# Down weights by output columns, the embedding's projection among the last quad's gate and up products

## The chip, the cores and the metric

The kernel runs on one core of one Trainium2 chip, in f32 throughout. The metric is device time in microseconds of one execution of the whole program.

## The reference

Two blocks follow each other on 256 tokens of width 1024. The first has two layers; the second, one layer with a recurrent unit, sparse attention and an MLP, is not touched. Cut to what the change bears on:

```python
def first_block(x, p, ...):
    for i in range(2):                                 # DEPTH
        h = rms_norm(x, norm_mix[i])
        q, k, v, cu, cg, ga, gb = split(h @ w_in[i])
        ...                                            # attention, convolution, gates
        x = x + merged @ w_out[i]
        h2 = rms_norm(x, norm_ffn[i])
        x = x + hier_moe(h2, ..., w_exp_gate[i], w_exp_up[i], w_exp_down[i])
        g_ple = sigmoid(rms_norm(x, norm_ple[i]) @ w_ple_gate[i])
        x = x + g_ple * (p[i] @ w_ple_proj[i])
    return rms_norm(x, norm_final)

def expert_block(xb, e):                               # inside hier_moe, 32 experts, FF = 512
    return (silu(xb @ w_gate[e]) * (xb @ w_up[e])) @ w_down[e]
```

The MoE's sum over experts has to be complete before the embedding's gate can be computed, since the gate takes a norm of x over all 1024 columns. The projection `p @ w_ple_proj` hangs on nothing but its weights.

## The kernel before

**The stream.** Every weight comes through one queue of transfers, issued by SP in one fixed order (`plan`, `Slabs`; `Store.issue`, L500 to 533). A slab is 2 MB (128 rows of 4096 f32); there are 12 places for slabs in SBUF (six called `ring`, five in `l_extra`, one `late`). A slab goes into a place as soon as the products that read the place's former slab have signalled, and PE waits for a slab where it first uses it. Some slabs are issued as pairs, 4 MB at once.

**The MoE.** The 32 experts are done in 8 quads of four; each expert has 32 slots of tokens, so that one product of a quad uses a 32-column piece of TensorE for each expert. A quad takes 12 slabs. Eight are for gate and up (`gate_up`, products at L1633: 128 rows of D each, 512 columns of gate and 512 of up for each expert). PE then transposes the hidden activations (L1679), and four down slabs follow (`down`, L1645). A down slab holds 128 of the 512 rows of FF for all 1024 output columns, so the result of a quad is complete only with the fourth slab; it is summed in two PSUM banks. ACT copies the left bank (L1724), DVE the right one (L1743), and PE's `combine` (L1623) spreads the slots back over the tokens, in four pieces of two products, which DVE adds to x (`add_part`, L1581). Within a quad the combine of the quad before is put behind the first gate and up slab. Quads 0 to 3 of a layer are computed in one block of the program together with the layer's front; quads 4 to 7 open the next block.

**The embedding's gate.** Behind the last quad, `ple_tensor` computes the gate in four banks of 16 products (L734 for the first three, L794 for the last, in two halves), with the mean square for the norm (L723) behind the first. Its left operand is x times the norm's gain (`scale_by_gain`, L750, DVE, buffer `late`), and the root of the mean is applied afterwards. The projection, from a slab of 1280 KB, has four banks of 8 passes (L734, from `l_extra`), which stand between the down slabs of the last quad. The stream's order at the end of a layer is: gate and up slabs of the last quad, projection slab, four down slabs, two gate slabs (2 MB each), slabs of the next stage.

**Behind the gate.** DVE takes each piece of the gate: times the root (L840), sigmoid by ACT (L816), times the projection (L843, read from PSUM), added to x (L846), times the gain of the norm that follows (L854 behind the second layer). Behind the first layer, layer 1's front follows in the same block (`q`, L875). Behind the second layer, seven filler products (`keep_busy`, L716) and the second block of the program (L2105).

Names in the rows: `ps` is PSUM, `hB` and `l_work` are scratch buffers in SBUF, `xT` is x transposed, `l_extra` and `ring` hold slabs.

Of the kernel before, what the change touches and what calls it, by code (L numbers as in the profile page):

```python
# [274 lines left out]
MOE_SLABS = QUADS * QUAD_SLABS  # L275
SLAB = 4096
# [5 lines left out]
class Slabs:  # L282
# [39 lines left out]
    def expert(self, layer, m):  # L322

        if m < CYCLE:
            return self.first[layer, "moe"] + self.sooner[layer].index(m)
        return self.first[layer, "moe"] + m + (m >= MOE_SLABS - FC)
# [9 lines left out]
def plan():  # L336
# [3 lines left out]
    for l in range(DEPTH):  # L340
# [55 lines left out]
def weight_stream(a):  # L396
# [13 lines left out]
    for l in range(DEPTH):  # L410
# [12 lines left out]
        dn = np.asarray(a["w_exp_down"][l]).reshape(QUADS, QUAD, FC, P, D).transpose(0, 2, 3, 1, 4)  # L423
# [153 lines left out]
class Layers:  # L577


    def __init__(self, nc, ctx, keep, store, lpar, edges, most):  # L580
# [50 lines left out]
        self.sq = dict(ple=self.hB, mix=extra[:, 1, 0:2048].rearrange(three, c=DC), ffn=work[:, 0:2048].rearrange(three, c=DC))  # L631
# [7 lines left out]
        self.y_slots = flat_b[:, DC * P:2 * DC * P]  # L639
        self.hid_slots = self.y_slots[:, 0:FF]  # L640
# [5 lines left out]
        for stage, bs in dict(ple=(0, 1, 4, 5), mean_ple=(7,), ple_gate=(2, 3, 6, 7, 2),  # L646
# [4 lines left out]
            for i, b in enumerate(bs):  # L651
# [12 lines left out]
         self.hidT_ready, self.y_left, self.y_right, self.part_filled, self.part_added, self.y_half, self.idle_set, self.x_half, self.gate_used, self.turned_back, self.over_landed,  # L664
# [5 lines left out]
             "hidT_ready", "y_left", "y_right", "part_filled", "part_added", "y_half", "idle_set", "x_half", "gate_used", "turned_back", "over_landed",  # L670
# [20 lines left out]
    def claimer(self, pe):  # L691
        last_in = {}

        def claim(stage, i):

            b = self.banks[stage, i]
            if b in last_in:
                s, n = last_in[b]
                pe.wait_ge(self.emptied[s], n + 2 if n == 3 and s == "ple" else n + 1)
# [81 lines left out]
    def ple_tensor(self, pe, claim, layer):  # L781
# [7 lines left out]
        w = store.wait(pe, i + 1)  # L789
        self.fill_bank(pe, claim, "ple_gate", 2, w, 0, self.hA, DC)  # L790
        for m in range(2):
            out = claim("ple_gate", 3 + m)
            for k in range(DC):
                mm = self.nc.tensor.matmul(out[:, 0:T], w[:, k, (2 + m) * P:(3 + m) * P], self.hA[:, k, :],  # L794
                                           start=(k == 0), stop=(k == DC - 1))
            mm.then_inc(self.filled["ple_gate"], 1)
        store.free(i + 1, self.filled["ple_gate"], 5)

    def gated_piece(self, n):

        m0, m1 = (2 * n, 2 * n + 2) if n < 3 else (n + 3, n + 4)
        b = min(n, 3)
        return slice(m0, m1), self.bank("ple_gate", n)[:, 0:(m1 - m0) * T], self.bank("ple", b)[:, (m0 - 2 * b) * T:(m1 - 2 * b) * T]

    def ple_scalar(self, act, step, then_norm):
        for b in range(4):
            act.wait_ge(self.part_added, 4 * (QUADS - SPLIT - 1) + b + 1)
# [2557 lines left out]
```

## Time and profile before

| | us |
|---|---|
| median of three runs | 1925.87 (1923.22, 1925.87, 1926.55) |
| profiled execution | 1927.43 |
| its span | 1925.70 |
| PE busy | 1654.3 (86%), 8204 instructions |
| PE weight loads busy | 946.4 (49%) |
| DVE busy | 733.5 (38%) |
| ACT busy | 365.8 (19%) |
| transfers | 564.73 MB, mean 293 GB/s |
| mean granted clock of TensorE | 0.930 of full speed |

A row of a timeline has the start in us, the length in us, the engine, the line, the operation and its tiles, with a count where equal instructions follow each other, and in brackets the engine's idle time ahead of it and what ended that. A product in f32 counts as two passes. PE's ends are modelled, so that a row may reach a little into the next one.

### The profile page before, as it was taken

The numbers are of one execution on the slowest core, as the hardware profiler recorded it, in microseconds if no ns is written. First come the engines' busy times: TensorE is split into PE (matmuls) and PEld (weight loads), VectorE is DVE, ScalarE is ACT, GpSimd is POOL, SyncE is SP. The second block draws the span as 40 slices with busy tenths as digits, with TensorE's granted clock in tenths as the row PEclk, the third lists the DMA queues.
The fourth block names the chain that finished last, engine by engine and source line by source line (L and its number), as shares of the span: only waits on it lengthen the run. The fifth ranks groups of instructions, "written<-read, shape, count | busy, mean of one in ns | idle before, by whom it ended". The sixth has DMA issues, their size and how long they took to land. (4 is left out here: it accounts for less than half of the span.)

```text
span 1925.7 us, 19591 instructions
## 1 busy us (share of the span) xinstructions
PE 1654.3 (86%) x8204; PEld 946.4 (49%) x8204; DVE 733.5 (38%) x1263; ACT 365.8 (19%) x796; POOL 0.2 (0%) x4
## 2 busy tenths in 40 slices
PE   9999985666766999999765766769999999999999
PEld 8546532222222784475221322228888865474444
DVE  5984210001100479632110101005638457745554
ACT  2342200000000223412000000003044234312200
POOL 0000000000000000000000000000000000000000
PEclk9999998788878999999887878889999999999999
DMA  8447899999999853479999999993544523344442
GB/s 359 174 146 328 342 425 431 431 431 430 430 427 430 335 224 131 178 324 382 434 426 430 432 432 428 431 425 148 198 154 154 208 88 131 131 151 155 150 168 97
DMA packets 31628, 564.73 MB, mean 293 GB/s; under 512 B 3633, under 2 KB 4145, under 8 KB 5553
## 3 DMA queue, kind: packets, MB, share of 16 engines
q1 hardware_dynamic: 31536, 563.42, 71.2%
q8 instruction: 69, 1.13, 0.2%
q14 instruction: 23, 0.18, 0.0%
HBM read 562.36 MB, written 1.05 MB: 293 GB/s over the span
## 5 line engine op out<-in xcount | busy, mean ns | idle before, releaser
L1633 PE MATMUL ps<-ring,hB 128*32 128x512 f32 x1024 | 150.6, 741 | 100.8 <-DMA ring<-in_stream 100.8
L1633 PE MATMUL ps<-l_extra,hB 128*32 128x512 f32 x768 | 120.2, 770 | 57.4 <-DMA l_extra<-in_stream 55.5
L1633 PEld LDWEIGHTS ps<-ring,hB 128*32 128x32 f32 x1024 | 40.2, 132 | 195.8 <-issue 194.9
L1645 PE MATMUL ps<-ring,hB 128*32 128x512 f32 x512 | 83.4, 808 | 57.4 <-DMA ring<-in_stream 57.4
L734 PE MATMUL ps<-late,ring 128*128 128x256 f32 x576 | 125.3, 379 | 0.0
L734 PEld LDWEIGHTS ps<-late,ring 128*128 128x128 f32 x576 | 109.4, 190 | 14.9
L1743 DVE COPY hB<-ps 128x512 f32<-128x512 f32 x16 | 11.1, 692 | 277.3 <-PE ps L1645 277.3
L1741 DVE TENSOR_TENSOR hB<-ps,hB 128x512 f32<-128x512 f32 x16 | 11.1, 692 | 274.1 <-ACT hB L1716 274.1
L2105 PE MATMUL ps<-late,ring 128*128 128x256 f32 x512 | 111.5, 379 | 0.0
L2105 PEld LDWEIGHTS ps<-late,ring 128*128 128x128 f32 x512 | 97.3, 190 | 14.9 <-issue 1.9
L1299 DVE SCALAR_TENSOR_TENSOR l_extra<-l_extra,lpar 128x255 f32<-128x255 f32 (+14 forms) x240 | 101.7, 465 | 5.9 <-ACT l_extra L1155 2.6
L1633 PEld LDWEIGHTS ps<-l_extra,hB 128*32 128x32 f32 x768 | 29.7, 134 | 137.1 <-issue 134.2
L1601 PE MATMUL ps<-l_work 128*128 128x128 f32 x512 | 66.4, 285 | 18.4 <-issue 17.7
L1601 PEld LDWEIGHTS ps<-l_work 128*128 128x128 f32 x512 | 60.9, 196 | 41.8 <-issue 41.8
L1645 PEld LDWEIGHTS ps<-ring,hB 128*32 128x32 f32 x512 | 18.9, 142 | 118.8 <-DMA ring<-in_stream 69.7
L1645 PE MATMUL ps<-l_extra,hB 128*32 128x512 f32 x512 | 61.5, 620 | 13.8 <-ACT hB L1720 8.1
L2451 PE MATMUL ps<-ring,late 128*128 128x512 f32 x160 | 71.5, 592 | 0.0
L1623 PE MATMUL ps<-l_work,hB 128*128 128x256 f32 x256 | 63.3, 390 | 0.1
L1623 PEld LDWEIGHTS ps<-l_work,hB 128*128 128x128 f32 x256 | 45.7, 189 | 24.9 <-issue 19.6
L1581 DVE TENSOR_TENSOR xT<-xT,ps 128x512 f32<-128x512 f32 x64 | 44.0, 688 | 33.5 <-PE ps L1623 33.5
L1571 DVE TENSOR_TENSOR l_work<-const,l_place 128x256 f32<-128x256 f32 x16 | 6.8, 425 | 129.2 <-PE ps L1609 126.0
L1003 PE MATMUL ps<-ring,l_extra 128*128 128x512 f32 x128 | 55.9, 592 | 0.0
(462 smaller groups left out, 2353.6 us busy)
## 6 DMA issues: line engine op xcount, KB each, us to landing
ring<-in_stream SPq DMA_DIRECT2D x80, 2048.0 KB, 7.8
ring<-in_stream SPq DMA_DIRECT2D x40, 4096.0 KB, 52.2
l_extra<-in_stream SPq DMA_DIRECT2D x26, 4096.0 KB, 52.6
l_extra<-in_stream SPq DMA_DIRECT2D x28, 2048.0 KB, 38.7
late<-in_stream SPq DMA_DIRECT2D x16, 2048.0 KB, 48.8
ring<-in_stream SPq DMA_DIRECT2D x2, 2024.0 KB, 8.2
ring<-in_stream SPq DMA_DIRECT2D x2, 1664.0 KB, 6.7
ring<-in_stream SPq DMA_DIRECT2D x2, 1536.0 KB, 18.8
```

The lines of the kernel that those rows point to most:

```text
L734: mm = self.nc.tensor.matmul(out[:, m * T:(m + 1) * T], w[:, k, c * P:(c + 1) * P], src[:, k, :], start=(k == 0), stop=(k == kc - 1))
L1003: mm = nc.tensor.matmul(out[:], src[:, k, t * P:(t + 1) * P], w[:, k, h * BANK:(h + 1) * BANK], start=(k == 0), stop=(k == AC - 1))
L1299: i = vec.scalar_tensor_tensor(y, u[:, c, TAPS - 1:TAPS - 1 + T - lead], self.tap(c, at), y, ALU.mult, ALU.add)
L1581: self.nc.vector.tensor_tensor(x, x, self.ps[6 + k % 2][:], ALU.add).then_inc(self.part_added, 1)
L1601: mm = nc.tensor.matmul(side_banks[piece % 2][:, at:at + P], htok[:, t, k * P:(k + 1) * P], pick[:, t].rearrange("p j s -> p (j s)"), star ...
L1623: mm = nc.tensor.matmul(part_banks[b % 2][:, m * T:(m + 1) * T], y_slots[:, c * P:(c + 1) * P], put, start=True, stop=True)
L1633: mm = nc.tensor.matmul(out[js, :], x_slots[:, c, js], w[:, 0, j * D + at:j * D + at + FF], start=(c == 0), stop=(c == DC - 1))
L1645: mm = nc.tensor.matmul(y_banks[half][js, :], hidT[:, f, js], w[:, 0, j * D + half * BANK:j * D + (half + 1) * BANK], start=(f == 0), stop ...
L1741: vec.tensor_tensor(self.hid_slots, ps[1][:], self.hid_slots, ALU.mult).then_inc(self.hid_ready, 1)
L1743: vec.tensor_copy(self.y_slots[:, BANK:], ps[3][:]).then_inc(self.y_right, 1)
L2105: mm = nc.tensor.matmul(out[:, m * T:(m + 1) * T], w[:, k, (c0 + m) * P:(c0 + m + 1) * P], src[:, k, :], start=(k == 0), stop=(k == kc - 1))
L2451: mm = nc.tensor.matmul(out[:], left[:, k], right[:, k], start=(k == 0), stop=(k == 3))
```

## The change

The down weights are cut by output columns: a down slab holds all 512 rows of FF for 256 of the 1024 output columns, and its columns are complete when its products are. In the last quad of a layer ACT copies each 256 columns by themselves (`y_last`), and a combine pair follows (`combine_last`). In other quads the copies stay as they were, of two banks, and the combine too.

The projection slab moves ahead of the last four gate and up slabs in the stream (`PLE_FROM`); its four banks are computed behind those four slabs, and ACT copies them to SBUF (`keep_ple`).

The two gate slabs stay at the end of the stream, behind the last down slab, in fixed places. `ple_tensor` now holds the order of the end: down 2, combine 2, down 3, the first half of the gate's bank 0 (k 0 to 3), combine 3, the second half (k 4 to 7), mean, the other banks. DVE's additions, gain products and sums go by halves, and behind the gate DVE multiplies a piece by the root ahead of finishing the piece before it. In the q products of the front, k is the outer loop now.

```diff
@@ plan
+            if m == PLE_FROM:
+                s.add((l, "ple"), [place[single % CYCLE]], P, 1, PLE // P * (D + T), m0 + MOE_SLABS)
...
-        s.add((l, "ple"), [place[single % CYCLE]], P, 1, PLE // P * (D + T), m0 + MOE_SLABS)
         for m in range(single, MOE_SLABS):
             s.add((l, "moe"), [place[(m + 1) % CYCLE]], P, 1, SLAB, m0 + m)
-        tail = ring if l < DEPTH - 1 else range(3, RING)
-        for _ in range(2):
-            s.add((l, "ple_gate"), tail, P, DC, BANK)
+        for n in range(2):
+            s.add((l, "ple_gate"), [pairs[n]], P, DC, BANK, m0 + MOE_SLABS + 1 + n)
@@ ple_tensor
-        w = store.wait(pe, i)
-        self.fill_bank(pe, claim, "ple_gate", 0, w, 0, self.hA, DC, self.scaled["ple"])
+        def gate_part(b, ks):
+            w = store.wait(pe, i + b // 2)
+            pe.wait_ge(self.scaled["ple"], ks[-1] + 1)
...
+        down(2)
+        combine(2)
+        down(3)
+        gate_part(0, range(4))
+        combine(3)
+        gate_part(0, range(4, 8))
         self.mean_square(pe, claim, "ple")
-        self.fill_bank(pe, claim, "ple_gate", 1, w, 1, self.hA, DC)
+        gate_part(1, range(8))
         store.free(i, self.filled["ple_gate"], 2)
...
@@ ple_scalar
         for b in range(4):
-            act.wait_ge(self.part_added, 4 * (QUADS - SPLIT - 1) + b + 1)
+            if b >= 2:
+                act.wait_ge(self.slab_used, last * QUAD_SLABS + DC + b + 1)
+                self.nc.scalar.copy(self.y_last[:, b * T:(b + 1) * T], self.ps[2 + b % 2][:, T:2 * T])\
+                    .then_inc(self.y_part if b == 2 else self.y_left, 1)
+            act.wait_ge(self.part_added, 4 * last + b + 1)
             self.square_bank("ple", b)
@@ ple_vector
-        for b in range(5):
-            if b < 4:
+        for half in range(2):
+            for b in (2 * half, 2 * half + 1):
                 self.add_part(dve, added + b)
-            if b:
-                dve.wait_ge(self.part_added, added + b)
-                self.scale_by_gain(layer, "ple", range(2 * b - 2, 2 * b))
-        for b in range(4):
-            self.sum_bank(dve, step, "ple", b)
+                dve.wait_ge(self.part_added, added + b + 1)
+                self.scale_by_gain(layer, "ple", range(2 * b, 2 * b + 2))
+            if half:
+                dve.sem_inc(self.y_right, 1)
+            for b in (2 * half, 2 * half + 1):
+                self.sum_bank(dve, step, "ple", b)
...
+        gate_by_root(0)
+        for n in range(5):
...
+            if n < 4:
+                gate_by_root(n + 1)
@@ front_tensor, q
-        for m in range(2):
-            for k in range(DC):
...
+        for k in range(DC):
+            pe.wait_ge(self.scaled["mix"], k + 1)
+            if k == (0 if layer else DC // 2):
+                store.wait(pe, i)
+            for m in range(3 if layer else 2):
...
@@ moe_tensor, down
-            for half in range(2):
+            half, at = (c % 2, c // 2) if q == QUADS - 1 else (c // 2, c % 2)
+            out = y_banks[half][:, at * T:(at + 1) * T]
+            for f in range(FC):
                 for j in range(QUAD):
...
-                    mm = nc.tensor.matmul(y_banks[half][js, :], hidT[:, f, js], w[:, 0, j * D + half * BANK:j * D + (half + 1) * BANK],
+                    mm = nc.tensor.matmul(out[js, :], hidT[:, f, js], w[:, 0, j * D + f * T:j * D + (f + 1) * T],
@@ moe_tensor, gate and up loop
+                if q == QUADS - 1 and c >= DC - 4:
+                    b = c - DC + 4
...
+                    self.fill_bank(pe, claim, "ple", b, w, b, pT, PLE // P)
@@ moe_tensor, end of the last quad
+            for c in range(FC // 2 if q == QUADS - 1 else FC):
+                down(q, n, c)
+            if q == QUADS - 1:
+                combine_last(0)
+                combine_last(1)
@@ block, behind the second layer
-                        pe.wait_ge(self.emptied["ple_gate"], 2)
+                        pe.wait_ge(self.emptied["mean_ple"], 1)
                         self.keep_busy(self.ps[3], self.const[:, C_UPTO:C_UPTO + T], 7)
```

What this does to the order on the engines is seen best in rows. On PE, at the end of a layer's last quad, before (L1645 is a down product, L734 from `l_extra` the projection, L1623 the combine, L734 from `ring` the gate, L723 the mean; `landed` waits are for slabs):

```order
L734 MATMUL ps<-l_extra 128x256 x4
L1645 MATMUL ps<-l_extra,hB 32x512 [waits landed6]
L1645 MATMUL ps<-l_extra,hB 32x512 x7
L1623 MATMUL ps<-l_work,hB 128x256 [waits l_part_added,l_y_left,l_put_copied]
L1623 MATMUL ps<-l_work,hB 128x256
L1623 MATMUL ps<-l_work,hB 128x256 [waits l_part_added]
L1623 MATMUL ps<-l_work,hB 128x256
L1623 MATMUL ps<-l_work,hB 128x256 [waits l_part_added,l_y_right]
L1623 MATMUL ps<-l_work,hB 128x256
L1623 MATMUL ps<-l_work,hB 128x256 [waits l_part_added]
L1623 MATMUL ps<-l_work,hB 128x256
L734 MATMUL ps<-late,ring 128x256 [waits l_scaled_ple,landed0]
```

The same place now (L1692 is a down product, L1655 the combine, L800 the gate, L726 the mean):

```order
L1692 MATMUL ps<-ring,hB 32x256 [waits landed5]
L1692 MATMUL ps<-ring,hB 32x256 x15
L1655 MATMUL ps<-l_work,hB 128x256 [waits l_part_added,l_y_part,l_put_copied]
L1655 MATMUL ps<-l_work,hB 128x256
L1692 MATMUL ps<-l_extra,hB 32x256 [waits landed6]
L1692 MATMUL ps<-l_extra,hB 32x256 x15
L800 MATMUL ps<-late,ring 128x256 [waits l_scaled_ple,landed0]
L800 MATMUL ps<-late,ring 128x256 x7
L1655 MATMUL ps<-l_work,hB 128x256 [waits l_part_added,l_y_left,l_put_copied]
L1655 MATMUL ps<-l_work,hB 128x256
L800 MATMUL ps<-late,ring 128x256 [waits l_scaled_ple,landed0]
L800 MATMUL ps<-late,ring 128x256 x7
```

Three combine pairs have moved ahead of the last down slab, and the fourth stands between the two halves of the gate's first bank, behind the wait for the gate slab.

On DVE, behind the gate of layer 1, before (L840 times the root, L843 times the projection, L846 added to x, L854 times the gain; the last two pieces of five):

```order
L840 TENSOR_TENSOR l_extra<-ps,late 128x256 [waits l_filled_ple_gate]
L843 TENSOR_TENSOR l_extra<-l_extra,ps 128x256 [waits l_filled_ple,l_emptied_ple_gate]
L846 TENSOR_TENSOR xT<-xT,l_extra 128x256 [waits l_emptied_ple]
L854 TENSOR_SCALAR hB<-xT,edges 128x256 [waits l_x_plus]
L840 TENSOR_TENSOR l_extra<-ps,late 128x256 [waits l_filled_ple_gate]
L843 TENSOR_TENSOR l_extra<-l_extra,ps 128x256 [waits l_filled_ple,l_emptied_ple_gate]
L846 TENSOR_TENSOR xT<-xT,l_extra 128x256 [waits l_emptied_ple]
L854 TENSOR_SCALAR hB<-xT,edges 128x256 [waits l_x_plus]
```

Now, from the multiply by the root of the last piece on (L865, L875, L878 and L886 are the four steps):

```order
L865 TENSOR_TENSOR l_extra<-ps,late 128x256 [waits l_filled_ple_gate]
L875 TENSOR_TENSOR l_extra<-l_extra,l_work 128x256 [waits l_emptied_ple,l_emptied_ple_gate]
L878 TENSOR_TENSOR xT<-xT,l_extra 128x256 [waits l_ple_mixed]
L886 TENSOR_SCALAR hB<-xT,edges 128x256 [waits l_x_plus]
L875 TENSOR_TENSOR l_extra<-l_extra,l_work 128x256 [waits l_emptied_ple,l_emptied_ple_gate]
L878 TENSOR_TENSOR xT<-xT,l_extra 128x256 [waits l_ple_mixed]
L886 TENSOR_SCALAR hB<-xT,edges 128x256 [waits l_x_plus]
```

The last piece's first step, which waits for PE's last gate products, now stands ahead of three steps of the piece before it.

## Rows read from the trace of the kernel before

**Rows 1.** The page: busy tenths of PE and of DMA in 40 slices.
```profile
PE   9999985666766999999765766769999999999999
DMA  8447899999999853479999999993544523344442
```

**Rows 2.** Stretches at layer 0's end: busy us by engine, clock, DMA share, GB/s.
```profile
620.00:640.00 20.00, 16.53 (x103) 8.25 (x101) 1.38 (x2) 0.86 (x3) 0.00 (x0) 1.00 1.00 426
660.00:680.00 20.00, 20.00 (x94) 17.62 (x93) 9.35 (x19) 6.11 (x11) 0.00 (x0) 1.00 0.61 242
```

**Rows 3.** Timeline of PE, end of layer 0's last quad and the gate.
```profile
612.17 5.34 PE L1633 MATMUL ps<-l_extra,hB 128*32 128x512 f32 x32 [4.39 <-DMA l_extra<-in_stream]
...
623.12 1.99 PE L734 MATMUL ps<-l_extra 128*128 128x256 f32 x8
...
631.32 1.92 PE L1645 MATMUL ps<-ring,hB 128*32 128x512 f32 x16 [2.43 <-DMA ring<-in_stream]
...
636.21 1.92 PE L1645 MATMUL ps<-l_extra,hB 128*32 128x512 f32 x16 [1.04 <-DMA l_extra<-in_stream]
638.06 3.97 PE L1623 MATMUL ps<-l_work,hB 128*128 128x256 f32 x16
641.87 7.07 PE L734 MATMUL ps<-late,ring 128*128 128x256 f32 x32
648.77 1.03 PE L723 MATMUL ps<-hB,const 128*128 128x256 f32 x4
...
670.36 7.07 PE L875 MATMUL ps<-hB,ring 128*128 128x256 f32 x32
```

**Rows 4.** Timeline of PE, the same place of layer 1 and the next block.
```profile
1296.68 1.92 PE L1645 MATMUL ps<-l_extra,hB 128*32 128x512 f32 x16 [1.04 <-DMA l_extra<-in_stream]
...
1302.34 7.07 PE L734 MATMUL ps<-late,ring 128*128 128x256 f32 x32
...
1330.83 3.19 PE L716 MATMUL ps<-const 128*128 128x256 f32 x14
1334.90 5.42 PE L2105 MATMUL ps<-hB,ring 128*128 128x256 f32 x24 [0.89 <-PEq L482]
```

**Rows 5.** Transfers, last down slab, then gate slabs: issue; KB, us to landing.
```profile
581.33 0.33 SPq L527 DMA_DIRECT2D l_extra<-in_stream  x1
...
l_extra<-in_stream SPq DMA_DIRECT2D x1, 2048.0 KB, 54.8
...
596.23 2.04 SPq L533 DMA_DIRECT2D ring<-in_stream  x2
...
ring<-in_stream SPq DMA_DIRECT2D x1, 2048.0 KB, 44.8
```

**Rows 6.** Timelines of ACT and DVE behind layer 0's last down slab.
```profile
637.34 0.59 ACT L1724 COPY hB<-ps 128x512 f32<-128x512 f32 x1 [17.11 <-PE ps L1645]
...
639.23 0.69 DVE L1581 TENSOR_TENSOR xT<-xT,ps 128x512 f32<-128x512 f32 x1 [0.34 <-PE ps L1623]
...
640.70 0.61 DVE L750 TENSOR_SCALAR late<-xT,edges 128x256 f32<-128x256 f32 x2
```

**Rows 7.** Timeline of DVE: its last work behind layer 1's gate.
```profile
1332.85 0.41 DVE L854 TENSOR_SCALAR hB<-xT,edges 128x256 f32<-128x256 f32 x1
```

**Rows 8.** Timeline of PE at the start: q's second part.
```profile
11.19 5.42 PE L875 MATMUL ps<-hB,ring 128*128 128x256 f32 x24 [0.58 <-DMA ring<-in_stream]
```

**Rows 9.** The page: queue of instruction loads, packets, MB, share of 16 engines.
```profile
q8 instruction: 69, 1.13, 0.2%
```

**Rows 10.** Stretch behind the wait of 4.39 us (clock 0.50), PE's other waits.
```profile
614.00:616.00 2.00, 2.00 (x16) 0.81 (x12) 0.00 (x0) 0.00 (x0) 0.00 (x0) 0.50 1.03 437
...
969.43 3.64 PE L1633 MATMUL ps<-ring,hB 128*32 128x512 f32 x32 [3.38 <-DMA ring<-in_stream]
...
1204.78 5.88 PE L1633 MATMUL ps<-ring,hB 128*32 128x512 f32 x28 [3.29 <-DMA ring<-in_stream]
...
1263.12 3.64 PE L1633 MATMUL ps<-ring,hB 128*32 128x512 f32 x32 [3.45 <-DMA ring<-in_stream]
```

More of the change, by code:

```diff
@@ L325, in expert @@
             return self.first[layer, "moe"] + self.sooner[layer].index(m)
-        return self.first[layer, "moe"] + m + (m >= MOE_SLABS - FC)
+        return self.first[layer, "moe"] + m + (m >= PLE_FROM)
     def until(self, consumed):
@@ L698, in claim @@
                 s, n = last_in[b]
-                pe.wait_ge(self.emptied[s], n + 2 if n == 3 and s == "ple" else n + 1)
+                pe.wait_ge(self.emptied[s], n + 1)
             last_in[b] = (stage, i)
@@ L867, in front_tensor @@
             pe.wait_ge(store.opened, 16)
-        out = claim("q", 0)
-        for m in range(2):
-            for k in range(DC):
-                if m == 0:
-                    pe.wait_ge(self.scaled["mix"], k + 1)
-                    if k == (0 if layer else DC // 2):
-                        store.wait(pe, i)
-                mm = nc.tensor.matmul(out[:, m * T:(m + 1) * T], w[:, k, m * P:(m + 1) * P], self.hB[:, k, :], start=(k == 0), stop=(k == DC - 1))
-        mm.then_inc(filled["q"], 1)
+        outs = [claim("q", b) for b in range(2)]
+        for k in range(DC):
[3 more added lines that the diff above has]
+            for m in range(3 if layer else 2):
+                mm = nc.tensor.matmul(outs[m // 2][:, m % 2 * T:(m % 2 + 1) * T], w[:, k, m * P:(m + 1) * P], self.hB[:, k, :],
+                                      start=(k == 0 and m != 1), stop=(k == DC - 1 and m == 1))
+                if k == DC - 1 and m == 1:
+                    mm.then_inc(filled["q"], 1)
         if layer == 0:
@@ L879, in front_tensor @@
         self.mean_square(pe, claim, "mix")
-        self.fill_bank(pe, claim, "q", 1, w, 1, self.hB, DC)
+        for m in range(3 if layer else 2, 4):
+            for k in range(DC):
+                mm = nc.tensor.matmul(outs[1][:, m % 2 * T:(m % 2 + 1) * T], w[:, k, m * P:(m + 1) * P], self.hB[:, k, :],
+                                      start=(k == 0 and m == 2), stop=(k == DC - 1 and m == 3))
+        mm.then_inc(filled["q"], 1)
         store.free(i, filled["q"], 2)
@@ L1610, in turn_put, with combine_pair @@
             mm.then_inc(self.put_filled, 1)
+        def combine_pair(n, b, y):
+            k = 4 * n + b
+            if k >= 2:
+                pe.wait_ge(self.part_added, k - 1)
+            for m in range(2):
+                c = 2 * b + m
+                mm = nc.tensor.matmul(part_banks[b % 2][:, m * T:(m + 1) * T], y[:, c * P:(c + 1) * P], put, start=True, stop=True)
+            mm.then_inc(self.part_filled, 1)
         def combine(n):
@@ L1666, in moe_tensor @@
                     turn_put(n)
+                if q == QUADS - 1 and c >= DC - 4:
+                    b = c - DC + 4
+                    i = store.slabs.first[layer, "ple"]
+                    both = store.wait(pe, i)[:, 0]
+                    w = both[:, 0:PLE // P * D].rearrange("p (c n) -> p c n", c=PLE // P)
+                    pT = both[:, PLE // P * D:].rearrange("p (c n) -> p c n", c=PLE // P)
+                    if b == 1:
+                        pe.wait_ge(self.put_copied, n + 1)
+                    if b == 2:
+                        pe.wait_ge(self.y_left, n)
+                        pe.wait_ge(self.y_right, n)
+                    self.fill_bank(pe, claim, "ple", b, w, b, pT, PLE // P)
+                    if b == 3:
+                        store.free(i, self.filled["ple"], 4)
             if q == 0:
@@ L1680, in moe_tensor @@
             mm.then_inc(self.turned_hid, 1)
-            if q == QUADS - 1:
-                i = store.slabs.first[layer, "ple"]
-                both = store.wait(pe, i)[:, 0]
-                w = both[:, 0:PLE // P * D].rearrange("p (c n) -> p c n", c=PLE // P)
-                pT = both[:, PLE // P * D:].rearrange("p (c n) -> p c n", c=PLE // P)
-                self.fill_bank(pe, claim, "ple", 0, w, 0, pT, PLE // P)
             pe.wait_ge(self.hidT_ready, n + 1)
@@ L1714, in moe_scalar @@
             nc.scalar.copy(self.put, ps[4][:, 0:T]).then_inc(self.put_copied, 1)
+            if q == QUADS - 1:
+                for b in range(4):
+                    self.keep_ple(act, b)
             act.wait_ge(self.slab_used, n * QUAD_SLABS + DC)
@@ L1720, in moe_scalar @@
             nc.scalar.copy(flat(self.hidT), ps[5][:]).then_inc(self.hidT_ready, 1)
-            act.wait_ge(self.y_half, n + 1)
+            if q == QUADS - 1:
+                for c in range(2):
+                    act.wait_ge(self.slab_used, n * QUAD_SLABS + DC + c + 1)
+                    nc.scalar.copy(self.y_last[:, c * T:(c + 1) * T], ps[2 + c][:, 0:T]).then_inc(self.y_part, 1)
+                continue
+            act.wait_ge(self.slab_used, n * QUAD_SLABS + DC + 2)
             if n:
@@ L1724, in moe_scalar, with keep_ple @@
             nc.scalar.copy(self.y_slots[:, 0:BANK], ps[2][:]).then_inc(self.y_left, 1)
+    def keep_ple(self, act, b):
+        act.wait_ge(self.filled["ple"], b + 1)
+        self.nc.scalar.copy(flat(self.ple_kept[:, pair(b), :]), self.bank("ple", b)[:]).then_inc(self.emptied["ple"], 1)
     def moe_vector(self, dve, q0, q1, n0):
```

108 lines of the change are left out of this document (59 added, 49 removed).

## The prediction

> **What bounds the kernel now.** I read the 40 slices first: PE is busy nine tenths or more where DMA is not, and DMA is at nine tenths through the long plateaus where PE falls to five or seven [rows 1]. Those plateaus are the two MoE stages. A stretch of 20 us at the end of layer 0's MoE has the DMA share at 1.00 and PE at 16.53 of 20 us; 40 us later PE has 20.00 of 20 and DMA 0.61 [rows 2]. So inside a quad the weight stream sets the time, and behind the last down slab the chain goes over to PE. What this change is worth is read from that crossing alone. Call L the time at which PE starts on the last down slab: 636.21 us in layer 0, 1296.68 in layer 1 [rows 3, 4].
>
> In the PE timeline [rows 3] PE waits 2.43 and 1.04 us for the last two down slabs, then has no idle time behind L: down 3, combine (3.97 us), gate bank 0, mean, the rest of the gate, layer 1's q products at 670.36. The gate starts at L + 5.66 in both layers (641.87 - 636.21, 1302.34 - 1296.68) and takes 28.49 us, so it ends at L + 34.15 (670.36, and 1330.83 in layer 1). From then on PE stays busy, so a later gate is a later end, one for one; the second layer's stage hangs on slots that this PE work frees, so the shift of layer 0 is passed on whole.
>
> The deciding view is that of the transfers. The last down slab was issued at 581.33 us and landed 54.8 us later, at 636.13; the first gate slab was issued at 596.23 and landed 44.8 later, at 641.03 [rows 5]. The gate slab comes 4.9 us behind the last down slab. Before, the combine (with down 3: 5.7 us of PE work) covered those 4.9 us entirely, and gate bank 0 found its weights there. L itself belongs to the stream: the change moves the 1280 KB projection slab within it but leaves the bytes ahead of the last down slab, and those ahead of the gate slabs, as they were.
>
> **The change part by part.**
>
> *Down weights by output columns, three of four combines ahead of the last slab.* Each down slab now completes 256 output columns, so six of the eight combine products run before L. Down 2 lands about 4.9 us ahead of L (631.32, [rows 3]); 1.92 us of products, an ACT copy of about 0.6 us [rows 6], and two products of 0.86 us fit before L. A down slab now has 32 passes of half the length instead of 16. No row shows that shape. If the passes halve, it costs 1.92 us as before; if every pass cost as much as a long one, 3.84. Either is hidden: in a quad by the stream's 4.9 us a slab, behind L because PE must wait until L + 4.9 anyway. I take 0, bounds 0 and 0.
>
> *The embedding's projection among the last gate and up products.* Its four groups took 1.99 us each between down slabs [rows 3]. They now stand behind gate and up slabs, where PE waits 4.39 us a slab for DMA [rows 3], and four ACT copies with them. The last copy is ahead of the quad's silu, so down 0 starts some 3 us later than before; down 1 follows, and the stage is caught up before down 2 lands. Cost 0. SP issues the projection slab before a pair of moe slabs, so that pair waits in SP's queue behind the slot of the projection slab; the stream has some 45 to 55 us of transfers in hand at any time [rows 5], so nothing runs dry.
>
> *The new order behind L.* This is the term that counts. PE's order is now down 3, gate products k 0 to 3 of bank 0 (8 products), combine 3, gate products k 4 to 7, mean, the other banks. One product is 6.90/16 = 0.4315 us (641.87 to 648.77, 32 passes for 16 products [rows 3]), so 8 products take 3.45 and a combine pair 0.86. From L:
> 1. down 3 until + 1.9; PE then has nothing until the gate slab lands: + 4.88.
> 2. 8 products: + 8.33. Combine 3, queued behind them although its input has been there since about + 2.6: + 9.19.
> 3. DVE's add begins 0.31 us behind the pair (pair 0 ends 638.06 + 0.86, the add starts 639.23), takes 0.69, the two gain scales 0.61 [rows 3, 6]; with 0.1 for handoffs, an estimate: + 10.9. PE waits 1.7 us for this, since the k 4 to 7 products ask for all eight scaled chunks.
> 4. 8 products, mean 0.87, three banks of 6.905: + 14.35, + 15.2, + 35.95.
>
> That is 35.95 - 34.15 = **+1.8 us** in each layer, +3.6 in all. The combine that was cover before the gate slab is work behind it now, and one DVE round trip is exposed. The order pays only if the gate slab lands within about 3.1 us of L.
>
> *DVE's order behind the gate.* Layer 1's last gate bank ends at 1330.83; DVE's last gain multiply then ends at 1332.85 + 0.41, 2.43 us later [rows 4, 7]. Now the last half piece's multiply by the root goes ahead of the piece before it, so seven operations of about 0.42 us instead of four stand behind the last bank: about 3.3 us. Seven filler products hold PE for 3.19 us there anyway, and the next block's products start 4.07 us behind the gate [rows 4]. +0.35, bounds 0 and 0.9. In layer 0 nobody waits for it in that time: PE's q products of layer 1 need chunks that are ready early.
>
> *q with k outside.* At the start PE waits 0.58 us for the second part of the q slab; eight products now lie before that point instead of four, which which covers it [rows 8]. The front's next stretch hangs on DVE and ACT; gain 0 to 0.58, I take 0. In layer 1 the mean comes 3.45 us later and the products put ahead of it cover it: 0.
>
> *More instructions.* The MoE has 1,024 more passes of PE. The instruction queue moves 69 packets and 1.13 MB in all [rows 9], so some ten packets more, 0.15 MB: 0.3 us at 430 GB/s, bounds 0 and 1.5 us if one of them delays the slab that is waited for.
>
> Sum without the clock: 3.6 + 0.35 = **+3.9**.
>
> *The clock.* PE now has two gaps behind L, of 3.0 and 1.7 us, around 3.45 us of work, where before it had none. What such gaps do is in the MoE stages: a wait of 4.39 us is followed by 32 passes in 5.34 us [rows 3], with a granted clock of 0.50 (1.2 GHz) in the stretch behind it, and one of 3.29 us by 28 passes in 5.88, while waits of 3.38 and 3.45 us are followed by 32 passes in 3.64 [rows 10]; behind the waits of 2.43 and 1.04 us ahead of L the clock stays at 1.00 (2.4 GHz) [rows 2, 3]. One fall costs 5.34 - 3.64 = 1.7 us. Gaps of just over 3 us go both ways, PE's work ahead of this one is short, and a second gap follows at once. I give each layer a fall with six chances in ten: one of two is likeliest, +1.6 rounded down for what the second gap absorbs.
>
> [...]
>
> **Forecast.** +3.9 + 1.6 = +5.5 us. The profiled execution took 1927.43 us around a span of 1925.70, 1.6 above the median of the three runs, 1925.87. The sum is a difference of spans, so it is set on the median: **1931.4 us** (a profiled execution would give about 1932.9).
>
> **The rivals.**
> - *The clock holds in both layers*: +3.9, 1929.8 us. For it: the gaps of 3.38 and 3.45 us without a fall [rows 10].
> - *It falls in both*: +3.9 + 3.2 = +7.1, 1933.0 us. For it: two gaps close together, where the trace has only one gap a slab.
> - *The other side: the gate slab lands with, or close behind, the last down slab.* If it is there at L + 1.9, the eight products run at once, combine 3 ends at + 6.2, the scales at + 7.9, the gate at + 33.0: -1.15 a layer, with the tail's 0.35 some -2 in all, 1923.9 us. It decides from 3.1 us between the two landings. It needs the 16 engines to finish the gate slab early. Against it: 4.9 us of spacing, which is 2 MB at 430 GB/s, and a queue that is never empty. "DMA: Bandwidth & Descriptors", section "Two DMAs through the same engine are not ordered", in the Trainium skill allows a later transfer to be complete before an earlier one; the trace shows them in order of issue here.
> - *The moved work isn't hidden*, as L moves by a late pair or by short passes that cost more than their share with a half clock: up to +5 more, 1936.
>
> **How the numbers follow.** Clock falling once 0.40 (1931.4), twice 0.27 (1933.0), never 0.16 (1929.8), gate slab early or any other gain 0.11 (1923.9 and below), moved work not hidden 0.06. The range that holds 8 in 10 takes the three middle cases with their bounds: tail 0 to 0.9, start -0.6 to 0, fetches up to 1.5: 1926.5 to 1936.5. A measurement of this kernel can tell about 0.2%, 3.9 us, from no change. The never case sits on that edge: half of it, a small part of the once case (with the start's 0.6 gained and a small fall) and about a third of the early-slab case count as the same. Slower 0.66, same 0.27, faster 0.07.
>
> **What would show it.** In the PE timeline after each L: an idle time of about 3 us before the gate's first eight products, released by DMA, and one of about 1.7 us behind combine 3, released by DVE's scales; the gate's end at L + 36 or, with a fall, + 37.6; the granted clock of the 4 us behind the gate slab's landing. The combines 0 to 2 before L, the projection among the gate and up products with L unmoved (636 us, 1297 less the shift of layer 0). I am wrong if the gate slab lands within 3 us of L, if L moves by over 1 us of itself, or if PE has an idle time in the front behind the gate in which the shift is lost.

## Result and the profile after

| | before | changed |
|---|---|---|
| median | 1925.14 us (17 runs, 1922.18 to 1927.20) | 1928.83 us (17 runs, 1927.55 to 1931.94) |
| ratio to before | | 1.0021 (95%: 1.0015 to 1.0027) |
| profiled execution, span | 1927.43, 1925.70 us | 1930.61, 1928.80 us |
| granted clock | 0.930 | 0.928 |

The change costs 4.0 us by the ratio (2.9 to 5.2), 3.7 by the medians. The forecast was 5.5 us and a range that holds the result; the direction is right, the size by about a third too large.

The timeline of PE in the changed kernel, end of layer 0's last quad and the gate (L1692 down, L1655 combine, L800 gate, L726 mean); it answers to [rows 3]:

```profile
621.93 1.99 PE L737 MATMUL ps<-l_extra 128*128 128x256 f32 x8
625.83 0.66 PE L1742 MATMUL ps<-const,hB 128*128 128x128 f32 x4 [1.90 <-DVE hB L1810]
627.16 3.22 PE L1692 MATMUL ps<-l_extra,hB 128*32 128x256 f32 x32 [0.67 <-ACT hB L1779]
630.21 1.90 PE L1692 MATMUL ps<-ring,hB 128*32 128x256 f32 x32
...
637.47 1.93 PE L1692 MATMUL ps<-l_extra,hB 128*32 128x256 f32 x32
640.66 3.72 PE L800 MATMUL ps<-late,ring 128*128 128x256 f32 x16 [1.26 <-DMA ring<-in_stream]
644.22 1.03 PE L1655 MATMUL ps<-l_work,hB 128*128 128x256 f32 x4
646.77 3.69 PE L800 MATMUL ps<-late,ring 128*128 128x256 f32 x16 [1.52 <-DVE late L753]
650.30 1.03 PE L726 MATMUL ps<-l_extra,const 128*128 128x256 f32 x4
651.16 20.88 PE L800 MATMUL ps<-late,ring 128*128 128x256 f32 x96
671.88 10.52 PE L906 MATMUL ps<-hB,ring 128*128 128x256 f32 x48
```

And layer 1, which answers to [rows 4]:

```profile
1287.59 1.93 PE L1692 MATMUL ps<-l_extra,hB 128*32 128x256 f32 x32 [0.68 <-ACT hB L1779]
...
1296.61 1.93 PE L1692 MATMUL ps<-l_extra,hB 128*32 128x256 f32 x32
1301.11 5.41 PE L800 MATMUL ps<-late,ring 128*128 128x256 f32 x16 [2.56 <-DMA ring<-in_stream]
1306.35 1.03 PE L1655 MATMUL ps<-l_work,hB 128*128 128x256 f32 x4
1308.90 3.69 PE L800 MATMUL ps<-late,ring 128*128 128x256 f32 x16 [1.52 <-DVE late L753]
...
1334.01 3.19 PE L719 MATMUL ps<-const 128*128 128x256 f32 x14
1338.09 7.14 PE L2176 MATMUL ps<-hB,ring 128*128 128x256 f32 x32 [0.89 <-PEq L483]
```

Both idle times that were forecast are there: DMA ahead of the gate's first eight products (1.26 and 2.56 us, forecast 3.0), DVE's scales behind combine 3 (1.52, forecast 1.7). Before had neither. In layer 1 the eight products took 5.41 us instead of 3.72, and a stretch of the trace (length, then busy us by engine, then the granted clock: 0.50) shows half clock there:

```profile
1303.00:1305.00 2.00, 2.00 (x6) 1.56 (x6) 0.00 (x0) 0.00 (x0) 0.00 (x0) 0.50 1.04 442
```

The transfers (issue row of SP, then us to landing) put layer 0's last down slab at 581.81 + 53.9 = 635.7 us and its gate slab at 597.51 + 43.1 = 640.6, 4.9 us apart as in [rows 5]:

```profile
581.81 0.33 SPq L528 DMA_DIRECT2D l_extra<-in_stream  x1
...
l_extra<-in_stream SPq DMA_DIRECT2D x1, 2048.0 KB, 53.9
...
597.51 0.33 SPq L534 DMA_DIRECT2D ring<-in_stream  x1
...
ring<-in_stream SPq DMA_DIRECT2D x1, 2048.0 KB, 43.1
```

A measure that leaves out where the stream stands is the time from the gate slab's landing to the gate's end. Before it is 29.3 us in both layers (670.36 - 641.05; 1330.83 - 1301.52). Now it is 671.88 - 640.62 = 31.26 in layer 0 and 1334.01 - 1301.06 = 32.95 in layer 1: +1.95 for the order, in each layer, and +1.7 for the clock in one. That makes 5.6 us in this execution, and the spans differ by 3.1. The rest lies in a place that the change doesn't edit. The shift of 1.53 us behind layer 0's gate is passed on unchanged up to 864 us, where the routing ahead of layer 1's MoE begins; there the two kernels' PE rows differ by their clock. Before first, the changed kernel behind it:

```profile
866.59 3.65 PE L1107 MATMUL ps<-const,late 128*128 128x128 f32 x16
870.04 3.01 PE L716 MATMUL ps<-const 128*128 128x256 f32 x8
866.00:868.00 2.00, 2.00 (x11) 2.00 (x12) 1.23 (x9) 1.48 (x3) 0.00 (x0) 0.50 0.95 410
```

```profile
867.58 1.94 PE L1144 MATMUL ps<-const,late 128*128 128x128 f32 x16
869.36 1.89 PE L719 MATMUL ps<-const 128*128 128x256 f32 x8
866.00:868.00 2.00, 2.00 (x20) 2.00 (x20) 0.16 (x1) 0.47 (x2) 0.00 (x0) 1.00 0.85 352
```

The same products take 6.66 us at half clock and 3.83 at full. Of the profiles of the ten kernels below, three have 3.83 us at this place and seven 5.2 to 5.6, whatever was edited. So I take the 2.3 us that the shift loses here (+1.5 to -0.8 in the issue times of the stream) for the luck of two executions and not for a part of the change. The kernel before has one profile only, so its usual time at this place isn't known; the last two columns of the table below don't reach over it.

### The profile page after: what moved, and what is told of

It is laid out like the page before. It is cut to its first block and busy times, and to the rows that moved or that the text cites. A ratio compares the mean times of both kernels' runs of the same rounds, so it can differ in the third digit from the quotient of the medians.

```text
span 1928.8 us, 21673 instructions
## 1 busy us (share of the span) xinstructions
PE 1652.0 (86%) x9228; PEld 981.5 (51%) x9228; DVE 732.1 (38%) x1261; ACT 371.8 (19%) x810; POOL 0.2 (0%) x4
## 3 DMA queue, kind: packets, MB, share of 16 engines
q8 instruction: 77, 1.26, 0.3%
## 5 line engine op out<-in xcount | busy, mean ns | idle before, releaser
L1680 PE MATMUL ps<-ring,hB 128*32 128x512 f32 x1024 | 157.4, 769 | 106.8 <-DMA ring<-in_stream 106.8
L1680 PE MATMUL ps<-l_extra,hB 128*32 128x512 f32 x768 | 111.7, 719 | 42.7 <-DMA l_extra<-in_stream 40.8
L1680 PEld LDWEIGHTS ps<-ring,hB 128*32 128x32 f32 x1024 | 40.7, 136 | 205.2 <-issue 204.2
L1692 PE MATMUL ps<-ring,hB 128*32 128x256 f32 x1024 | 81.6, 487 | 63.6 <-DMA ring<-in_stream 63.6
L2176 PE MATMUL ps<-late,ring 128*128 128x256 f32 x512 | 111.5, 379 | 0.0
L2176 PEld LDWEIGHTS ps<-late,ring 128*128 128x128 f32 x512 | 97.3, 190 | 14.9 <-issue 1.9
L1692 PEld LDWEIGHTS ps<-ring,hB 128*32 128x32 f32 x1024 | 38.4, 139 | 105.7 <-DMA ring<-in_stream 69.4
L737 PE MATMUL ps<-late,ring 128*128 128x256 f32 x384 | 83.2, 379 | 0.0
L737 PEld LDWEIGHTS ps<-late,ring 128*128 128x128 f32 x384 | 73.0, 190 | 9.9
L1770 ACT COPY l_work<-ps 128x256 f32<-128x256 f32 x16 | 6.0, 373 | 358.4 <-PE ps L1646 358.4
L1692 PE MATMUL ps<-l_extra,hB 128*32 128x256 f32 x1024 | 61.8, 394 | 12.2 <-ACT hB L1779 9.5
L1655 PE MATMUL ps<-l_work,hB 128*128 128x256 f32 x256 | 63.7, 390 | 1.2 <-issue 1.1
L800 PE MATMUL ps<-late,ring 128*128 128x256 f32 x256 | 58.3, 388 | 6.9 <-DMA ring<-in_stream 3.8
L1655 PEld LDWEIGHTS ps<-l_work,hB 128*128 128x128 f32 x256 | 45.7, 189 | 24.3 <-issue 19.0
```

The costliest lines, as they stand in the source:

```text
L737: mm = self.nc.tensor.matmul(out[:, m * T:(m + 1) * T], w[:, k, c * P:(c + 1) * P], src[:, k, :], start=(k == 0), stop=(k == kc - 1))
L800: mm = self.nc.tensor.matmul(out[:, at:at + T], w[:, k, c * P:(c + 1) * P], self.hA[:, k, :], start=(k == 0 and at == 0), stop=(k == DC - ...
L1655: mm = nc.tensor.matmul(part_banks[b % 2][:, m * T:(m + 1) * T], y[:, c * P:(c + 1) * P], put, start=True, stop=True)
L1680: mm = nc.tensor.matmul(out[js, :], x_slots[:, c, js], w[:, 0, j * D + at:j * D + at + FF], start=(c == 0), stop=(c == DC - 1))
L1692: mm = nc.tensor.matmul(out[js, :], hidT[:, f, js], w[:, 0, j * D + f * T:j * D + (f + 1) * T], start=(f == 0), stop=(f == FC - 1))
L2176: mm = nc.tensor.matmul(out[:, m * T:(m + 1) * T], w[:, k, (c0 + m) * P:(c0 + m + 1) * P], src[:, k, :], start=(k == 0), stop=(k == kc - 1))
```

## Experiments

Theory A: the loss is the order behind the last down slab, combine 3 queued behind a wait for a slab that lands 4.9 us later. Rival B: the column cut or the projection's new place costs by itself. Theory C: the wait of PE there makes the clock fall. Times are against the kernel before on the same chip, by the ratio of runs with its 95% interval. "Landing to end" is the time, in layers 0 and 1 of the profiled execution, from the landing of the gate slab to the gate's end; in e4, e7, e6 and e9, where the gate slab comes first, from the landing of the last down slab, so that it always starts when both slabs are there. The last column is the sum of the two less that of before (29.3 twice).

| kernel | us against before | landing to end | sum less before |
|---|---|---|---|
| changed | +4.0 (2.9 to 5.2) | 31.26, 32.95 | +5.6 |
| e1 combine 3 first | +0.2 (-1.5 to 1.9) | 28.6, 28.6 | -1.35 |
| e2 fillers | +6.7 (4.0 to 9.4) | 32.4, 32.4 | +6.1 |
| e3 q in the old order | +3.9 (2.1 to 5.6) | 31.3, 31.3 | +3.9 |
| e5 silu first | +5.8 (3.5 to 8.3) | 31.3, 34.3 | +6.9 |
| e10 e5 with fillers | +4.2 (2.5 to 6.0) | 31.3, 31.3 | +3.9 |
| e8 e1 with silu first | +0.8 (-1.0 to 2.5) | 28.6, 30.3 | +0.35 |
| e4 gate slab ahead of down 3 | -1.9 (-3.7 to -0.2) | 28.0, 28.5 | -2.1 |
| e7 e4 with silu first | -2.7 (-4.6 to -1.0) | 27.9, 27.9 | -2.8 |
| e6 gate slab ahead of down 2 | -4.8 (-6.7 to -2.9) | 26.5, 28.1 | -4.0 |
| e9 e6 by smaller steps | -7.7 (-10.4 to -5.2) | 25.3, 25.7 | -7.6 |

In all ten experiments the last column lies inside the interval of the time: as far as these intervals can tell (1.7 to 2.7 us to either side), what the kernels gain and lose is gained and lost between the landing and the gate's end. Only the changed kernel's own profile lies above its interval, by the clock's fall in layer 1; without it the column would be +3.9.

**e1: combine 3 ahead of the gate.**

```diff
         down(3)
-        gate_part(0, range(4))
         combine(3)
+        gate_part(0, range(4))
         gate_part(0, range(4, 8))
```

> The changed kernel with combine 3 ahead of the gate's first eight products, nothing else. Theory A (the loss is the order behind the last down slab: combine 3 queued behind the wait for the gate slab, then one round trip over DVE): the idle time of 1.5 us behind combine 3 is gone, PE waits some 1.2 us (L + 3.4 to L + 4.7) for the gate slab, the gate ends at about L + 33.4 with L before's own 636.2 and 1296.7, the first eight gate products take 3.5 us in both layers (no clock fall behind so short a wait). Against the kernel before: -1.5 us (0 to -3). Rival B (the column cut or the projection's new place costs by itself): the end stays at +2 us or more against before.

Layer 0's timeline of PE:

```profile
635.54 1.93 PE L1692 MATMUL ps<-l_extra,hB 128*32 128x256 f32 x32
638.02 1.10 PE L1655 MATMUL ps<-l_work,hB 128*128 128x256 f32 x4 [0.54 <-issue]
639.55 7.17 PE L800 MATMUL ps<-late,ring 128*128 128x256 f32 x32 [0.43 <-DMA ring<-in_stream]
```

One moved line takes the whole loss back, with the column cut and the projection in their new places: rival B, which had to leave 2 us or more, is out. A cost of theirs of a microsecond or so isn't: landing to end is 1.35 us shorter than before in sum, and the time shows no gain, though its interval reaches -1.5. The waits of 1.2 us are 0.4 and 0.3, since PE is late for the last down slab: in layer 0 it landed at 634.6 us and PE began at 635.54.

**e2: five fillers in the wait**, `keep_busy(ps[4], ..., 5)` behind down 3.

> The changed kernel with five filler products (2.2 us of PE work) in the wait between down 3 and the gate's first eight products. If the clock falls because PE waits there (theory C), the first eight gate products take 3.5 to 3.7 us in both layers, where layer 1's took 5.4, and the time is 0.8 to 1.7 us below the changed kernel: +2.0 to +3.0 against before. If the fall has another cause (rival D), one layer's first eight products still take about 5.4 us and the time stays at +3.7. If the fillers reach past the landing of the gate slab, they cost up to 0.5 us a layer.

The first eight products take 3.62 us in both layers, as C has it, but the run doesn't decide, since the wait that was to make the clock fall is gone as well, and it costs 2.7 us more than the changed kernel: PE was late for down 3 by 2 us here in both layers, so that the fillers stood on the path. The premise of a 3 us wait was wrong. Why PE was late is in the rows of the changed kernel's layer 0: behind the last projection bank PE waits 1.90 and 0.67 us, and down 0 then takes 3.22 us instead of 1.93, at half clock:

```profile
627.00:629.00 2.00, 1.84 (x20) 0.92 (x24) 0.00 (x0) 0.11 (x1) 0.00 (x0) 0.50 0.94 401
```

In the kernel before PE had a bank of the projection between the transposes and down 0 and no wait there, and down 0 started 5.9 and 4.6 us earlier in the two layers:

```profile
621.26 1.92 PE L1645 MATMUL ps<-l_extra,hB 128*32 128x512 f32 x16
1283.02 1.92 PE L1645 MATMUL ps<-l_extra,hB 128*32 128x512 f32 x16
```

**e3: the old order of the q products.** `front_tensor` with the loop over k inside, as before.

> The changed kernel with the q products in the old order (k inside). Theory A: the time is that of the changed kernel (+3.7 us against before) within 0.5, since the 0.6 us that PE gains at the start is taken up by the wait for ACT and DVE at 92 us. Rival E (k outside is worth its 0.58 us, or costs something): +4.3, or +3.2 and less.

+3.9 against +4.0; intervals of this width can't tell 0.6 us, but the rows can. In the changed kernel PE's gain at the start ends in a wait for ACT, and e3, without that wait, has the same products no later (the changed kernel first, e3 behind it). So q's order is worth nothing here:

```profile
91.84 0.52 PE L988 MATMUL ps<-const,l_extra 128*128 128x128 f32 x3 [0.86 <-ACT l_extra L1225]
```

```profile
91.76 0.52 PE L983 MATMUL ps<-const,l_extra 128*128 128x128 f32 x3
```

**e5: silu ahead of the projection's last copy.** ACT's queue has the copy of the projection's last bank ahead of the quad's silu, and that copy waits for PE's products. Of the edit ACT's part is shown; PE's wait for the same copy moves from the transposes to down 0.

```diff
-                for b in range(4):
+                for b in range(3):
                     self.keep_ple(act, b)
...
             nc.scalar.activation(self.hid_slots, ps[0][:], ACT.Silu).then_inc(self.gu_silu, 1)
+            if q == QUADS - 1:
+                self.keep_ple(act, 3)
```

> The changed kernel with ACT's silu of the last quad ahead of its copy of the projection's last bank (and PE's wait for that copy moved from the transposes to down 0). Theory C (the changed kernel hides part of its loss in a half-clock down 0, since ACT's copy ahead of the silu leaves PE idle for 1.9 and 0.7 us there): down 0 starts some 2 us earlier and takes 1.9 us at full clock in both layers, PE is at the last down slab when it lands, and then waits 2.5 to 3.0 us for the gate slab in both layers, with the first eight gate products at 5.2 to 5.5 us behind it. The stage starts earlier and ends later: +1 us (0 to +2) against the changed kernel, +4 to +6 against before. Rival G (an earlier down 0 is time gained): 1 to 4 us below the changed kernel.

PE in e5, layer 0 and layer 1:

```profile
624.36 1.93 PE L1692 MATMUL ps<-l_extra,hB 128*32 128x256 f32 x32 [0.77 <-ACT l_work L1797]
...
634.73 1.93 PE L1692 MATMUL ps<-l_extra,hB 128*32 128x256 f32 x32 [1.28 <-DMA l_extra<-in_stream]
639.63 3.72 PE L800 MATMUL ps<-late,ring 128*128 128x256 f32 x16 [2.96 <-DMA ring<-in_stream]
...
1300.73 6.76 PE L800 MATMUL ps<-late,ring 128*128 128x256 f32 x16 [2.96 <-DMA ring<-in_stream]
```

Down 0 begins 1.2 us behind the last projection bank's end instead of 3.2, and at full clock; the wait ahead of the gate is 2.96 us in both layers, which is what the prediction had for the changed kernel. The clock holds in layer 0 and falls in layer 1, which costs 3.0 us. The time isn't 1 to 4 us below the changed kernel's, as rival G had it, so G is out; that it is above it (+5.8 against +4.0) is within the two intervals. I had expected a fall in both layers; one of the two had none.

**e10: e5 with the five fillers.**

> e5 (silu first, PE in time for the last down slab) with five filler products, 2.2 us, in the wait of 3.0 us between down 3 and the gate's first eight products. Theory C (the wait makes the clock fall): the wait that is left is 0.6 to 0.9 us, the first eight products take 3.6 to 3.8 us in both layers, where e5 has 6.8 in layer 1, and the time is 1.5 to 3 us below e5: +3.3 to +4.8 against before, its gate 31.2 us behind the gate slab's landing in both layers. Rival D (the fall has another cause): a first-eight time of over 5 us in one layer, and +6 as e5.

```profile
637.27 2.42 PE L719 MATMUL ps<-const 128*128 128x256 f32 x10
640.20 3.72 PE L800 MATMUL ps<-late,ring 128*128 128x256 f32 x16 [0.50 <-DMA ring<-in_stream]
...
1297.66 2.43 PE L719 MATMUL ps<-const 128*128 128x256 f32 x10
1300.69 3.72 PE L800 MATMUL ps<-late,ring 128*128 128x256 f32 x16 [0.60 <-DMA ring<-in_stream]
```

With PE in time the fillers are hidden, the wait is 0.5 to 0.6 us, and the eight products take 3.72 us in both layers. Work without any use in the wait is worth about 1.6 us against e5, though the intervals overlap; in the trace the 3.0 us fall is gone. This supports C and doesn't show it: e5's own layer 0 had no fall without any filler, so both layers of e10 may have held by chance.

**e8: e1 with silu first.**

> The changed kernel with combine 3 ahead of the gate's first products (as e1) and ACT's silu first (as e5). Theory A: PE is in time for the last down slab, combine 3 is done at L + 3.5, PE waits 1.4 us for the gate slab, no clock fall, and the gate ends 28.6 us behind the gate slab's landing, as in e1: within 0.7 us of e1, -0.5 to -1.5 against before. Rival G (PE's lateness cost e1 something): 1.5 us or more below e1, -2 and less against before.

No better than e1, so PE's lateness cost e1 nothing that can be measured; A's gain of 0.5 to 1.5 us didn't show. Layer 0 is as expected (landing to end 28.6), and in layer 1 the clock fell all the same, behind three shorter waits in a row (1.31, 0.54 and 1.32 us):

```profile
1299.11 8.86 PE L800 MATMUL ps<-late,ring 128*128 128x256 f32 x32 [1.32 <-DMA ring<-in_stream]
```

Layer 0 has 7.17 us in that row, with nearly the same waits (1.32, 0.54 and 1.31 us).

**e4 and e7: the first gate slab ahead of the last down slab.** The plan adds the gate slab ahead of slab 95, and PE's order is

```diff
         down(2)
         combine(2)
+        gate_part(0, range(4))
         down(3)
-        gate_part(0, range(4))
+        gate_part(0, range(4, 6))
         combine(3)
-        gate_part(0, range(4, 8))
+        gate_part(1, range(6))
+        gate_part(0, range(6, 8))
...
```

> The changed kernel with the first gate slab ahead of the last down slab in the stream, and PE's order: down 2, combine 2, gate bank 0 k 0 to 3, down 3, bank 0 k 4 to 5, combine 3, bank 1 k 0 to 5, bank 0 k 6 to 7, mean, bank 1 k 6 to 7, the rest. Theory A: with the gate slab there first (at 636 and 1296 us) and the down slab 4.9 us later, PE has work in every gap, so the idle times of 1.3 and 1.5 us in layer 0 and of 2.6 and 1.5 in layer 1 go, and layer 1's clock fall of 1.7: 7 to 8 us below the changed kernel, -4 us against before (-2 to -6). Rival F (the last down slab, 4.9 us later, ends the chain: what hangs on combine 3 is exposed): PE waits for it or for DVE behind it by over 2 us a layer, 0 to +3 against before.

> The kernel with the gate slab ahead of the last down slab alone (e4), and silu first as in e5. Theory A: down 0 is 2 us earlier and at full clock, but PE then waits for the gate slab (1 to 2 us) and for the last down slab (1 to 1.5 us), so the end stays: 0 to -1 us against e4, -2.6 to -3.6 against before. Rival G (the time of down 0 was on the path): -6 against before.

Both are faster than before, e4 by half of the 4 us that I had expected, at the edge of its range. In e4 PE has no wait from 635.67 us on in layer 0, and from 1294.06 in layer 1, until the gate's end; but down 0 runs at half clock in both layers (3.22 and 3.59 us), and PE comes to the gate slab 1.7 and 2.0 us behind its landing. Silu first (e7) turns down 0's time into waits for slabs, 1.32 and 1.19 us in layer 0, as expected, and changes the end by less than the intervals tell.

**e6 and e9: the gate slab ahead of the last two down slabs**, silu first, gate products between the down slabs; e9 takes the first of them by two k at a time, so that they start when two chunks are scaled instead of four. PE's order in e9, against the changed kernel:

```diff
+        gate_part(0, range(2))
+        gate_part(1, range(2))
+        gate_part(0, range(2, 4))
         down(2)
+        gate_part(1, range(2, 3))
         combine(2)
+        gate_part(1, range(3, 4))
         down(3)
-        gate_part(0, range(4))
+        gate_part(0, range(4, 6))
         combine(3)
-        gate_part(0, range(4, 8))
+        gate_part(1, range(4, 6))
+        gate_part(0, range(6, 8))
...
```

> The first gate slab ahead of the last two down slabs, silu first as in e5, and PE's order: combine 0 and 1, gate bank 0 k 0 to 3, down 2, bank 1 k 0 to 1, combine 2, bank 1 k 2 to 3, down 3, bank 0 k 4 to 5, combine 3, bank 1 k 4 to 5, bank 0 k 6 to 7, mean, bank 1 k 6 to 7, the rest. Theory A (what counts is PE work that is left when the last slab lands): PE has no wait of over 1 us from the gate slab's landing (about 631 and 1291 us) on and the gate ends 34 to 35 us behind that landing, 4 to 5 us earlier than in the kernel before: -7 us against before (-4 to -10). Rival F (the last two down slabs, 4.9 us later each, become the end): waits of over 2 us ahead of down 3 or behind combine 3, and no better than the kernel with one down slab behind the gate slab, -2.6.

> e6 with the gate's first products by smaller steps: bank 0 k 0 to 1, bank 1 k 0 to 1, bank 0 k 2 to 3 ahead of down 2, then one k of bank 1 on either side of combine 2. Theory A (PE's idle time behind combine 1, 1.91 us while DVE adds and scales, is on the path in both layers): it falls to 0.5 us or less, and with it layer 1's clock fall there (5.4 instead of 3.7 us): 3 us below e6 (2 to 4.5), -8 us against before. Rival F (a slab or DVE is waited for instead): new waits of over 1 us ahead of down 2 or combine 2, and less than 1 us of gain.

e6 kept a wait of 1.91 us for DVE's scales, and in layer 1 a clock fall behind it (5.38 us for eight products), so its gate ended later than I had put it, 36 and 38 us behind the gate slab's landing instead of 34 to 35, and the time is -4.8 instead of -7. e9's rows of layer 1:

```profile
1285.61 5.42 PE L801 MATMUL ps<-late,ring 128*128 128x256 f32 x24 [0.66 <-DVE late L754]
1290.96 1.93 PE L1699 MATMUL ps<-ring,hB 128*32 128x256 f32 x32
1292.82 1.13 PE L801 MATMUL ps<-late,ring 128*128 128x256 f32 x4
1293.79 1.03 PE L1662 MATMUL ps<-l_work,hB 128*128 128x256 f32 x4
```

From here to the gate's end PE has no wait, and twelve products take 5.42 us, full clock. e9 beats both kernels, as expected (-8): 1915.44 us, ratio 0.996 (0.9946 to 0.9973). The last down slab lands 4.9 us later than in the changed kernel, relative to the stream, and nobody waits for it.

## Why the prediction was nearly right

- **The new order behind L: right.** Terms forecast and measured, layer 0: eight products 3.45 and 3.56 (640.66 to 644.22), combine 3 0.86 and 1.03, the wait for DVE 1.7 and 1.52, and +1.8 us a layer against +1.95 by landing to end. e1 shows that it is the whole loss. The short passes cost half of a long one, as taken: 32 of them in 1.93 us.
- **The gate slab's landing: right.** 4.9 us behind the last down slab in every profile with this order of the stream; the rival in which it comes early didn't occur.
- **"The stage is caught up before down 2 lands": wrong.** The prediction had down 0 start 3 us later than before. It started 5.9 us later in layer 0 (627.16 us) and 4.6 in layer 1 (1287.59), against the rows of before at e2. The 4.39 us that it counted "a slab" stand ahead of a pair (32 passes, [rows 3]). PE began down 3 1.7 us (layer 0) and 0.4 us (layer 1) behind its landing, so that layer 0's L stands at 637.47 instead of 636.21: a move of over 1 us, one of the signs of being wrong that the prediction named, though the slab itself landed 0.4 us earlier. The prediction saw the last copy ahead of silu, but not that PE would be idle behind the projection and that the clock would fall there: before, the projection's products stood in just that place. It cost nothing only because of the later wait for the gate slab: silu first brings no gain, neither on the changed kernel (e5) nor on e1 (e8).
- **The clock: a fall came, in another place than forecast.** It is the term that was mis-sized, 1.6 us forecast. The forecast rested on a wait of 3.0 us and six chances in ten a layer. The changed kernel's waits were 1.26 us in layer 0, without a fall, and 2.56 in layer 1, with one of 1.7 us. In e3, which is the changed kernel there, both are short (1.27 and 0.86) and neither fell. Between down 0 and the gate's end the clock fell once in each of these four layers, but in three of them already at down 0 (3.22 us in the changed kernel, 3.19 and 3.53 in e3), where the lost time went out of the wait for the gate slab and cost nothing. Without a fall behind that wait the sum is 2 x 1.95 = 3.9 us, with one 5.6; the measured 4.0 (2.9 to 5.2) lies at the rival in which the clock holds, with a part of executions that fall. That this rival's own sum was 3.9 too is in part luck: its order was 0.15 us a layer too small and its 0.35 for DVE's tail wasn't there. e5, in which the wait is what I had assumed, costs 5.8. How many executions of the changed kernel have a fall can't be counted from times alone; that stays open, and so does whether the wait alone makes it.
- **By the Trainium skill** ("TensorE: Matmul & The Clock Gate", "HAM oscillation"), in a kernel whose bursts of products are shorter than the waits for DMA between them, every burst starts at half clock. The runs agree in part, with bursts that are the longer ones: e5 has the same 2.96 us wait ahead of eight products (3.72 us at full clock) in two layers, and one fall.
- **DVE's order behind layer 1's gate: 0.35 forecast, 0 measured.** DVE ends 3.11 us behind the gate, and PE's fillers of 3.19 us still end last; the gap to the next block is 0.89 us, as in [rows 4].
- **q and the start: right at 0** (e3's rows). **The extra instruction loads** have no visible price: 77 packets instead of the 69 of [rows 9], and the gate slabs land 0.4 us earlier than before.
- **The shift of layer 0 passed on whole: right as far as the routing,** where the clock, 2.3 us between two profiles, covered it. e1's layer 0 ends 3.7 us earlier than the changed kernel's, and its layer 1 gate slab lands 3.0 us earlier.

## What to carry to other kernels

Ahead of a wait for a transfer goes every piece of work whose input is already there; a short piece queued behind that wait costs itself and the round trips that hang on it. Where a stage waits for a stream, look at the order of the stream before the cut of the work: here a slab whose products can run in the gaps, put ahead of the ones that end a chain, gave 7.7 us (e9), and the new cut showed no gain (e1). And work that looks hidden may be what fills an engine's gap in its place, as the projection did between the transposes and down 0, so look at that before moving it out. To read a tail like this one, take the time from the last landing to the end of the stage: it leaves out where the stream stands and agreed with the times of all ten experiments.

## What the hardware showed that I had not expected

The granted clock fell to half (1.2 GHz) behind waits far shorter than the 3 us gaps of [rows 10], where several stood close together: behind 1.90 and 0.67 us in the changed kernel's layer 0 (down 0 in 3.22 us, though not in layer 1, 1.93), and behind 1.31, 0.54 and 1.32 us in e8's layer 1, though not in its layer 0. The two waits of 1.90 and 0.67 us stand in both layers of five kernels (the changed one, e1 to e4); in seven of these ten layers down 0 took 3.2 to 3.6 us, in three 1.93. One fall cost between 1.3 us (that down 0) and 3.0 us (e5). And the same products of the routing, with PE busy ahead of them by its rows, took 3.83 us in the changed kernel's profile and 6.66 in that of before, by the clock alone.
